# Two-layer hybrid decoder step: memory values stream past held probabilities, one held linear-attention state serves two heads, state updates read their own 32 rows

## The reference, cut to what matters

```python
# linear attention (GLA), one chunk of 8 tokens per sample, 4 heads, dk = 32, dv = 64
a = where(mask, einsum('bthk,bshk->bhts', qt, kt), 0)
o = einsum('bhts,bshv->bthv', a, vc) + einsum('bthk,bhkv->bthv', qt, S)      # S: the sample's own state

# SSD state update, 2 groups, state 128
h = h * exp(cs[:, -1]) + einsum('bsh,bshp,bshn->bhpn', wend, xc, Bc)

# memory attention, 4 heads of 64 over the sample's own 256 memory tokens
p = softmax(einsum('blhd,bmhd->bhlm', q, mem_k) * scale)
o = einsum('bhlm,bmhd->blhd', p, mem_v)                                      # then @ mem_wo
```

## Time and profile before

| | |
|---|---|
| timed runs, median (range) | 1595.49 us (1595.32 to 1599.95) |
| the profiled execution's span | 1593.4 us |
| difference of the two | 2.1 us |
| TensorE busy | 1530.4 us, 96% |
| DVE, ACT, POOL busy | 737.1, 457.6, 258.1 us |
| mean granted TensorE clock | 0.957 of full |
| DMA | 174.47 MB, 109 GB/s on average |

### The profile page before, as it was taken

The page is one execution under the profiler, slowest core; times in us unless marked ns, Lnnn a source line. Parts: engine busy times, 40 slices in busy tenths (PEclk is TensorE's granted clock), DMA queues, the critical chain, the costliest instruction groups (busy, mean ns, idle before and its releaser), DMA issues.

```text
span 1593.4 us, 20211 instructions
## 1 busy us (share of the span) xinstructions
PE 1530.4 (96%) x6544; PEld 1073.1 (67%) x6544; DVE 737.1 (46%) x1446; ACT 457.6 (29%) x997; POOL 258.1 (16%) x494
## 2 busy tenths in 40 slices
PE   7988889999999999999999878999999999999999
PEld 5656656666777777777766655666668677777776
DVE  1345648788414344330014456488883243443300
ACT  1246335545213111110013372355541131111100
POOL 2000244332022100001100003333320220000000
PEclk9999879999988999999999998799998989999999
DMA  6330424333034344333443213233320343343332
GB/s 243 122 94 0 182 79 124 104 94 100 1 122 148 119 124 128 119 104 113 153 132 109 80 62 147 81 115 101 106 72 31 115 150 119 122 129 120 114 110 93
DMA packets 83627, 174.47 MB, mean 109 GB/s; under 512 B 12642, under 2 KB 51075, under 8 KB 82627
## 3 DMA queue, kind: packets, MB, share of 16 engines
q1 hardware_dynamic: 73872, 163.55, 31.9%
q0 software_dynamic: 9504, 9.19, 2.0%
q10 hardware_dynamic: 146, 0.44, 0.1%
HBM read 166.84 MB, written 6.29 MB: 109 GB/s over the span
## 4 chain that ended last, share of the span: by engine, by line
PE 89%; DVE 6%; ACT 3%; issue 1%; DMA 0%; SPq 0%; DVEq 0%
PE bank L443 34%; PE bank L783 14%; PE bank L1008 12%; PE bank L884 4%; PE bank L814 4%; PE bank L787 3%; PE bank L790 2%; PE bank L861 1%; PE bank L983 1%; PE bank L756 1%; ACT area L1564 1%; ACT area L1556 1%; PE bank L993 1%; PE bank L672 1%; PE bank L994 1%
## 5 line engine op out<-in xcount | busy, mean ns | idle before, releaser
L443 PE MATMUL bank<-xg,slot 128*128 128x320 f32 x2048 | 559.2, 434 | 9.2 <-DMA slot<-in_weights 9.2
L443 PEld LDWEIGHTS bank<-xg,slot 128*128 128x128 f32 x2048 | 390.1, 191 | 173.7 <-DMA slot<-in_weights 9.2
L1772 ACT ACTIVATE sq<-bank 128x512 f32<-128x512 f32 x256 | 151.7, 592 | 171.4 <-PE bank L783 163.9
L1364 DVE TENSOR_REDUCE small<-sq 128x8 f32<-128x512 f32 x256 | 169.3, 682 | 62.3 <-ACT sq L1772 59.9
L1008 PE MATMUL bank<-area,slot 128*128 128x320 f32 x704 | 189.8, 432 | 0.0
L1008 PEld LDWEIGHTS bank<-area,slot 128*128 128x128 f32 x704 | 133.8, 190 | 55.7
L1914 POOL DMA_DIRECT2D krT<-in_cache_r x256 | 127.3, 497 | 233.9 <-issue 224.6
L1564 ACT ACTIVATE area<-area 128x336 f32<-128x336 f32 (+4 forms) x112 | 63.2, 566 | 333.4 <-DVE area L1513 300.8
L1456 DVE TENSOR_TENSOR x<-x,bank 128x320 f32<-128x320 f32 x48 | 23.4, 487 | 270.6 <-PE bank L1008 174.8
L783 PE MATMUL bank<-wuk_nat,area 128*128 128x512 f32 x320 | 145.3, 597 | 0.0
L1901 POOL TENSOR_SCALAR xg<-x,par 128x320 f32<-128x320 f32 x48 | 58.4, 1224 | 289.6 <-DVE x L1456 283.6
(11 more groups left out here) (322 smaller groups left out, 1782.9 us busy)
## 6 DMA issues: line engine op xcount, KB each, us to landing
slot<-in_weights SPq DMA_DIRECT2D x216, 512.0 KB, 3.6
area<-in_cache SPq DMA_DIRECT2D x160, 128.0 KB, 2.1
kept<-in_cache SPq DMA_DIRECT2D x96, 128.0 KB, 2.1
slot<-in_weights SPq DMA_DIRECT2D x18, 384.0 KB, 4.2
krT<-in_cache_r POOLq DMA_DIRECT2D x256, 16.0 KB, 2.1
xg<-in_ssd_t SPq DMA_DIRECT2D x2, 1024.0 KB, 4.8
area<-in_ssd_n SPq DMA_DIRECT2D x2, 1024.0 KB, 13.1
hs_out<-area POOLq DMA_DIRECT2D x2, 1024.0 KB, 4.1
```

The source lines that it names most:

```text
L443: last = mm(out[:, 0:T], w[:, k, :], xg[:, k, :], start=(k == 0), stop=(k == KD - 1))
L1364: dve.tensor_reduce(ssk[:, t % 2, 8 * j:8 * j + 8], ksq[k % 3], AX.X, ALU.add).then_inc(V.fire(on["k_summed"]), 1)
L1772: f(ksq[k % 3], b[:, :].rearrange("p (h d) -> p h d", h=HEADS), ACT.Square).then_inc(A.free("key", l, t, j), 1)
```

## The change

Four edits.

1. `ssd_states`: the matmul for samples 0 to 3 contracts rows 0 to 31 and the one for samples 4 to 7 rows 32 to 63, where before both contracted 64.
2. `gla`, prompt part: for each pair of heads (0 and 2, then 1 and 3) one matmul holds `gst` and streams 128 columns, in place of one of 64 columns per head. The four L740 come first. As two heads now share a result, only the first head of a 64-row block starts the accumulation.
3. `gla`, sample part: for each sample and pair of heads one matmul of 16 columns (two strided pieces of 8), 16 in all where there were 32 of 8 columns; the samples are the outer loop, so that the two halves of the PSUM rows alternate. The four L752 stand in front.
4. Memory values: the held operand is now the probabilities, 32 columns (4 heads x 8 queries of one sample), and the values stream, 256 columns. Each sample writes its own 32 PSUM rows; four samples fill a bank, two banks instead of one. The result has queries on partitions, so it is copied to `mos` by ACT, transposed by TensorE (two 128 x 128 per bank, into "score" banks) and then copied by ACT in eight pieces of 64 rows x 32 columns into `mo`.

```diff
--- before.py
+++ after.py
@@ -334,6 +334,7 @@
         mp = [view(M + 6912 + i * 512, 512, "p (s m) -> p s m", s=2) for i in range(5)]
         mpt = [view(M + 10456 + i * 512, 512, "p (s i m) -> p s i m", s=2, i=2) for i in range(2)]
         mo = view(M + 2304, 2 * T, "p (r t) -> p r t", r=2)
+        mos = view(M + 2944, 512, "p (f c) -> p f c", f=2)
 
         hff = view(0, NFF * T, "p (j t) -> p j t", j=NFF)
         ubuf = [view(M + i * 340, UPAD) for i in range(2)]
@@ -689,8 +690,9 @@
                 for half in range(2):
                     b = banks.open("proj", "hs", l, g, half)
                     pe.wait_ge(*banks.before("hs", l, g, half))
-                    mm(b[:, :], xw[0:TS, 2, g * P:(g + 1) * P],
-                       bm[0:TS, 4 * half:4 * half + 4, g * P:(g + 1) * P], **F).then_inc(banks.full("hs", l, g, half), 1)
+                    rows = slice(32 * half, 32 * half + 32)
+                    mm(b[:, :], xw[rows, 2, g * P:(g + 1) * P],
+                       bm[rows, 4 * half:4 * half + 4, g * P:(g + 1) * P], **F).then_inc(banks.full("hs", l, g, half), 1)
 
             def ssd_norm(l):
 
@@ -738,10 +740,10 @@
                     for h in range(4):
                         r, g = 64 * (h % 2), h // 2
                         last = mm(b[r:r + 64, g * 64:(g + 1) * 64], tok[:, i, 512 + h * 64:576 + h * 64],
-                                  dec[:, i, h, at:at + 64], start=True, stop=(c == 0))
-                        if c:
-                            last = mm(b[r:r + 64, g * 64:(g + 1) * 64], gst, qtm[:, h, c * 64:(c + 1) * 64],
-                                      start=False, stop=True)
+                                  dec[:, i, h, at:at + 64], start=(g == 0), stop=(c == 0 and g == 1))
+                    for hh in range(2 if c else 0):
+                        last = mm(b[64 * hh:64 * hh + 64, 0:P], gst, qtm[:, hh::2, c * 64:(c + 1) * 64],
+                                  start=False, stop=True)
                     last.then_inc(banks.full("o", l, c), 1)
                 pe.wait_ge(*banks.emptied("a", l, 2))
                 pe.wait_ge(gsb_in, 16 * (l + 1))
@@ -750,10 +752,11 @@
                 for h in range(4):
                     r, g = 64 * (h % 2), h // 2
                     mm(b[r:r + 64, g * 64:(g + 1) * 64], tok[0:TS, 2, 512 + h * 64:576 + h * 64],
-                       dec[0:TS, 2, h, 0:TS], start=True, stop=False)
-                    for s in range(NB):
-                        at = g * 64 + NQ * s
-                        last = mm(b[r:r + 64, at:at + NQ], gsb[:, s, :], qtm[:, h, TP + NQ * s:TP + NQ * s + NQ],
+                       dec[0:TS, 2, h, 0:TS], start=(g == 0), stop=False)
+                for s in range(NB):
+                    for hh in range(2):
+                        out = b[64 * hh:64 * hh + 64, 0:P].rearrange("p (g t) -> p g t", g=2)[:, :, NQ * s:NQ * s + NQ]
+                        last = mm(out, gsb[:, s, :], qtm[:, hh::2, TP + NQ * s:TP + NQ * s + NQ],
                                   start=False, stop=(s == NB - 1))
                 last.then_inc(banks.full("o", l, 4), 1)
                 pe.wait_ge(*on["vm_ready"].at(l))
@@ -970,20 +973,27 @@
                         last.then_inc(banks.full("mo", l, v), 1)
                     if u == 6:
                         pe.wait_ge(*banks.emptied("mpt", l, 4))
-                        b = banks.open("mix", "mo", l, 4)
-                        pe.wait_ge(*banks.before("mo", l, 4))
                         for s2 in range(4):
-                            w = slot("cv", s2, "mo", l, 4).rearrange("p (s i c) -> p s i c", s=2, i=2)
-                            for s1 in range(2):
-                                s = 2 * s2 + s1
-                                for r in range(2):
-                                    at = (2 * s + r) * 16
-                                    for i in range(2):
-                                        q0 = 32 * (s % 4) + 16 * r
-                                        last = mm(b[:, at:at + 16], w[:, s1, i, r * P:(r + 1) * P],
-                                                  mpt[0][:, s // 4, i, q0:q0 + 16], start=(i == 0), stop=(i == 1))
-                        last.then_inc(banks.full("mo", l, 4), 1)
-                pe.wait_ge(*banks.emptied("mo", l, 4))
+                            w = slot("cv", s2, "mo", l, 4 + s2 // 2).rearrange("p (s i c) -> p s i c", s=2, i=2)
+                            if s2 % 2 == 0:
+                                b = banks.open("mix", "mo", l, 4 + s2 // 2)
+                                pe.wait_ge(*banks.before("mo", l, 4 + s2 // 2))
+                            for i in range(2):
+                                for s1 in range(2):
+                                    row = 32 * (2 * (s2 % 2) + s1)
+                                    last = mm(b[row:row + 32, 0:256], mpt[0][:, s2 // 2, i, row:row + 32],
+                                              w[:, s1, i, :], start=(i == 0), stop=(i == 1))
+                            if s2 % 2:
+                                last.then_inc(banks.full("mo", l, 4 + s2 // 2), 1)
+                        for f in range(2):
+                            pe.wait_ge(*banks.emptied("mo", l, 4 + f))
+                            b = banks.open("score", "mot", l, f)
+                            pe.wait_ge(*banks.before("mot", l, f))
+                            for r in range(2):
+                                last = pe.transpose(b[:, r * P:(r + 1) * P], mos[:, f, r * P:(r + 1) * P], cc("ident"))
+                            last.then_inc(banks.full("mot", l, f), 1)
+                for f in range(2):
+                    pe.wait_ge(*banks.emptied("mot", l, f))
                 for half in range(2):
                     w = slot("mwo", half, "mwo", l, 4 * half + 3).rearrange("p (m k c) -> p m k c", m=4, k=2)
                     for mi in range(4):
@@ -1838,13 +1848,19 @@
                         b = banks.of("mo", l, v)
                         act.wait_ge(*banks.filled("mo", l, v))
                         copy(mo[:, v // 2, (v % 2) * P:(v % 2) * P + P], b[:, 0:P]).then_inc(A.free("mo", l, v), 1)
-                b = banks.of("mo", l, 4)
-                act.wait_ge(*banks.filled("mo", l, 4))
-                for hh in range(2):
-                    rows = slice(64 * hh, 64 * hh + 64)
-                    src = b[rows, 0:256].rearrange("p (b r c) -> p r b c", b=NB, r=2)[:, :, :, 8 * hh:8 * hh + 8]
-                    ins = copy(mo[rows, :, TP:T].rearrange("p r (b q) -> p r b q", b=NB), src)
-                    ins.then_inc(A.step(), 1) if hh == 0 else ins.then_inc(A.free("mo", l, 4), 1)
+                for f4 in range(2):
+                    b = banks.of("mo", l, 4 + f4)
+                    act.wait_ge(*banks.filled("mo", l, 4 + f4))
+                    copy(mos[:, f4, :], b[:, 0:256]).then_inc(A.free("mo", l, 4 + f4), 1)
+                for f4 in range(2):
+                    b = banks.of("mot", l, f4)
+                    act.wait_ge(*banks.filled("mot", l, f4))
+                    for r in range(2):
+                        for hh in range(2):
+                            rows, at = slice(64 * hh, 64 * hh + 64), TP + 32 * f4
+                            src = b[rows, r * P:(r + 1) * P].rearrange("p (b h q) -> p b h q", b=4, h=4)[:, :, 2 * r + hh, :]
+                            ins = copy(mo[rows, r, at:at + 32].rearrange("p (b q) -> p b q", b=4), src)
+                            ins.then_inc(A.free("mot", l, f4) if (r, hh) == (1, 1) else A.step(), 1)
 
             def mlp(l):
                 for j in range(NFF):
```

## The result

The changed kernel took **1567.01 us** (median, 1566.49 to 1569.65) against 1595.40 for the kernel before, run beside it. The ratio is 0.9822, 95% interval [0.9807, 0.9837]: faster by 28.4 us. Predicted were 1566, range 1562 to 1573.

The account below looks back on a forecast made before the run. TensorE, busy for 96% of the span, was taken to bound the kernel. Gains of 12.8 + 13.0 + 3.6 + 0.2 = 29.6 us took the span from 1593.4 to 1563.8, plus 2.1: 1566 us, range 1562 to 1573.

Parts of the forecast that it names:

- Sample part: Linear attention, L752 to L763: 2.43 us instead of 8.82, a gain of 6.4 per layer, 12.8 in all.
- Memory values: First value matmul to output projection: 4.27 us instead of 10.76, a gain of 6.5 per layer, 13.0 in all.
- Rival C: Matmuls keep program order: first part of memory values 3.7 us instead of 1.97, 1.7 a layer, 1569.4; chance 0.10.
- Clock at the output projection: Clock stays up after the memory values, so the projection's head gains 1.8 us per layer, 3.6 in all.
- Rival B: Clock drops in the memory part all the same, one layer or both: 1.8 us a layer, 1567.7 to 1569.4; chance 0.24.
- State updates: Row halves run side by side, but DVE's chain limits the gain to 0.1 us per layer, 0.2 in all.
- Prompt chunks: Linear attention, chunks 1 to 3: equal columns per half, so gain 0, bounds plus or minus 0.1 us per chunk.
- Both move together: Cache part: page loads from group 2 on move with TensorE's dense matmuls, so no new wait, cost 0.
- my list of signs that would refute me: L984 at 3.7 us or more, L759 over 3, clock 0.50 in L1003, or new TensorE waits in the cache part.
- Rise of the clock: After the sample part, clock returns 3.3 us after dense matmuls begin, as before; bounds 1.7 us loss, 0.4 gain per layer.
- D: Rival: clock rises later after the sample part, 1.7 us a layer lost, up to 1569.4; chance 0.13.
- F: Rival: low-clock stretches elsewhere shorten as everything moves, one to two shorter by 3 us: 1563; chance 0.08.

Follow-up runs that it names:

- experiment 4: Changed kernel with the sample part's state matmuls written half by half, all samples of one column half before the other; 1571.32 us, one execution.
- experiment 5: Kernel before, sample part with score matmuls first and state matmuls alternating column halves, still 8 columns per head; 1589.88 us, one execution.
- experiment 3: Kernel before, value matmuls streaming the same 16 columns four times (64 columns), same loads and output; 1586.20 us, ratio 0.9941.
- Experiment 1: Kernel before with the memory-values edit alone; 1579.65 us, ratio 0.9893.
- experiment 7: Kernel before with the prompt part of the linear attention edit alone; 1594.40 us, one execution.
- Experiment 10: Also called mask_and_stores: changed kernel with the value mask on DVE in two halves and stores mk_out, mv_out before the krT loads; 1559.53 us, ratio 0.9769.
- experiment 8: Changed kernel with POOL's stores mk_out and mv_out issued before its 16 krT loads instead of after; 1565.57 us, ratio 0.9794.
- experiment 9: Changed kernel with linear attention's value mask computed by DVE in two halves instead of by POOL; 1563.07 us, ratio 0.9786.

## Why the prediction was right, step by step

- **Sample part.** 12.8 predicted, 12.75 measured. The price by turns of two halves held: L759's 32 instructions took 1.89 (predicted 1.8), L754 to L759 0.62 (0.63). Experiments 4 and 5 show the reason as well as the number: it is the order that alternates the halves.
- **Memory values.** 13.0 predicted, 13.16 measured: L984 1.96, as L946; the estimated ACT copy was 0.193 us instead of 0.21. Some 2.7 us of the 6.6 per layer is clock that L983 had lost (experiment 3), which the prediction took from rows without naming it. Rival C, matmuls held to program order at 3.7 us, did not happen. The overlap depends on the order: quarters in turns of two or four instructions overlap, halves in turns of 16 mostly don't (experiment 4). The Trainium skill ("TensorE: Matmul & The Clock Gate", Part 3) has matmuls start and end in program order, and weight loads overlap matmuls in flight only where row groups differ. The trace does not agree: the tiles of L984 share all rows and differ in columns, and still 32 instructions of 256 columns took 1.96 us.
- **Clock at the output projection.** 3.6 predicted, 3.58 measured. Rival B had 0.24 and did not happen. That 488 to 496 stayed at 1.00 was the right row to go by: the new part has the same shape. Experiment 1 shows that edit 4 alone keeps the clock up, and experiment 3 that the narrow streams had made it fall.
- **State updates.** 0.2 predicted, 0.4 measured. The matmuls gave 0.59 of the 0.86 us, as row halves overlapped only in part, and the wait behind DVE's chain took 0.39 back. The two state additions on DVE came down to 1.29 us, where I had 1.38 as the floor:

```profile
199.05 1.29 DVE L1244 TENSOR_TENSOR area<-area,bank 128x512 f32<-128x512 f32 x2 [0.69 <-PE bank L694]
```

- **Prompt chunks.** 0 predicted, 0.58 measured, at the end of my bounds. A mis-sized term: 0.15 a layer is the edit (experiment 7), and the rest is the clock, which fell at 206.9 instead of 206.6, 0.2 us into the restarted chunks.
- **"Both move together", cost 0.** This step failed in layer 0: 1.07 us were given back, 0.70 of them as TensorE's wait for the fourth page of group 2. It was on my list of signs that would refute me. SP's issue did move with TensorE: the fourth load stands 3.55 us behind the first, 3.51 before. The mis-sized term is the landing. I took it from the median of 2.1 us over the whole stage; the page issued at 227.01 took 3.2. SP's loads moved by 6.7 us, but POOL's krT loads and its first two stores stand where they stood (224.34, before 224.35), and the other two moved by 4.1 us only. The first of these two, in the kernel before and in the changed one:

```profile
229.70 0.54 POOL L1918 DMA_DIRECT2D mk_out<-mk  x1
```

```profile
225.64 0.54 POOL L1934 DMA_DIRECT2D mk_out<-mk  x1
```

  Before, these stores stood beside the first page load (230.15), and the first three pages took 2.5 to 2.9 us and the fourth 2.1. Now they stand beside the third and fourth, which took 3.4 and 3.2. Experiment 10 makes the stores a part of it, experiment 8 leaves it open; the rest is open too.
- **Rise of the clock.** 3.3 us after L773 predicted. L776 started at 216.97 and the clock rose at 220.5: 3.5 to 3.6, about 0.1 us of loss in each layer; D did not happen. Neither did F: the stretch of 435.3 to 452.3 stands at 428.8 to 445.8 now, as long as before. What I had not listed is a new low stretch of 3.4 us in layer 1 (+0.71) and a shift of others against the work. The named terms gave 30.5 us, 0.9 more than predicted; all other stages together cost 1.9, cache included. Hence 28.6 instead of 29.6. The case that happened is the forecast, with one small new wait. That the total came within 1 us is in part luck: 0.9 us more than predicted from the named terms stand against 1.9 us of losses that the prediction did not have.

## What to carry to other kernels

Where each matmul streams fewer columns than its load holds, swap the operands or let one load serve two heads, and write the matmuls so that neighbours fall in different column groups of the array; here, in the sample part, the order alone was worth more than halving the instructions (4.68 us against 1.69). Look at the granted clock behind such a stretch too, since nearly empty streams slowed the dense matmuls that followed. After a gain on TensorE, look at once for transfers issued by an engine that did not move with it, and take their landing from that stretch and not from a median over the stage.

## What the hardware showed that I had not expected

- In L983 the clock fell with 16 columns per load, and with 64 columns and the same loads it stayed at 1.00 (experiment 3). Yet in mask_and_stores it stayed at 0.50 from 425 to 441.8, through 16.8 us of mostly 64-column matmuls with PE busy for 16.44.
- Two DVE instructions, L1313, took 3.77 us beside POOL's 3.62 us multiply, against 1.01 without it. The first ended at 205.16, 0.35 us after the multiply in the changed kernel:

```profile
201.19 3.62 POOL L1970 TENSOR_TENSOR area<-area,const 64x2048 f32<-64x2048 f32 x1
```

  The Trainium skill ("SBUF — State Buffer", Who interferes with whom) tells of a port pair shared by DVE and GpSimd, held as an exclusive lock, at which a DVE instruction with two SBUF inputs contends with a GpSimd instruction that reads SBUF. The trace agrees, and the time could be had back: 2.75 us a layer (experiment 9).
- The same instructions differ by up to several us with the clock that they happen to meet: 2.45, 1.85 or 1.42 for the sample part, 4.6 more in one cache part. An edit of this size is to be read by its stage and not by the total.
